# Dilated and grouped-query attentions: values as the stationary operand, probabilities moving, two heads in two column halves

## What is computed

```python
s = jnp.einsum('bhgqk,...')          # scores, query x key
p = jax.nn.softmax(s, axis=-1)       # divided by the row sum
o = jnp.einsum('bhgqk,bkhd->bqhgd', p, v)
```

## Time and profile before

| | us |
|---|---|
| median of 3 runs (2414.51 to 2415.35) | 2415.19 |
| the profiled execution, own time | 2413.57 |
| its span | 2411.8 |
| dilated attention, first scores to the next product | 875.0 to 979.2 |
| grouped-query attention, the same | 1553.2 to 1627.9 |

### The profile page before, as it was taken

One profiled execution on the slowest core, in us unless ns is written; L12 is line 12 of the kernel. 1 busy time (PEld: TensorE's weight loads), 2 busy tenths in 40 slices (PEclk: granted clock), 3 DMA queues, 4 the chain that ended last, 5 costly groups with the idle time before them and its releaser, 6 DMA issues.

```text
span 2411.8 us, 30157 instructions
## 1 busy us (share of the span) xinstructions
PE 2257.6 (94%) x11002; PEld 1858.1 (77%) x11002; DVE 1302.4 (54%) x1964; ACT 1106.8 (46%) x1646; POOL 54.1 (2%) x70
## 2 busy tenths in 40 slices
PE   7998899999999998999999998799999859999994
PEld 6876788888888876788888877678888648888883
DVE  3555663333365344453333477442355469898996
ACT  3435363433433246262442353352324348888884
POOL 1000000000000000000000000000000010000001
PEclk8999999999999999999999999999999979999997
DMA  5220233333223310243323232103323179999995
GB/s 167 88 79 27 79 105 97 97 97 98 91 79 96 96 45 1 79 130 97 96 87 105 79 116 82 60 1 105 96 70 105 57 284 397 409 410 408 407 404 188
DMA packets 129139, 338.60 MB, mean 140 GB/s; under 512 B 10528, under 2 KB 11712, under 8 KB 129040
## 3 DMA queue, kind: packets, MB, share of 16 engines
q1 hardware_dynamic: 117744, 296.85, 35.4%
q0 software_dynamic: 7840, 27.59, 3.4%
q10 hardware_dynamic: 3456, 12.81, 1.3%
HBM read 320.96 MB, written 16.25 MB: 140 GB/s over the span
## 4 chain that ended last, share of the span: by engine, by line
PE 84%; DVE 8%; ACT 4%; issue 1%; DMA 1%; POOL 0%; SPq 0%; ACTq 0%; DVEq 0%; POOLq 0%
PE bank L2136 40%; PE bank L2139 18%; PE bank L2485 10%; PE bank L2522 5%; PE bank L2243 3%; PE bank L2233 2%; PE bank L2223 2%; ACT arena L833 1%; DVE w_l L1261 1%; PE bank L2160 1%; PE bank L2465 1%; ACT w_h L795 1%; DMA X<-in_x_dram 1%; DVE stat L1293 1%; DVE xt_l L1328 1%
## 5 line engine op out<-in xcount | busy, mean ns | idle before, releaser
L1261 DVE TENSOR_TENSOR w_l<-w_raw,w_h 128x1024 fp32r<-128x1024 f32 x370 | 447.6, 1222 | 615.0 <-ACT w_h L795 612.0
L795 ACT CAST w_h<-w_raw 128x1024 fp32r<-128x1024 f32 x370 | 385.5, 1051 | 746.1 <-PE bank L2136 523.6
L2136 PE MATMUL bank<-w_h,xt_h 128*128 128x512 f32 (+1 forms) x960 | 378.9, 395 | 16.5 <-DVE w_l L1261 7.5
L2136 PE MATMUL bank<-w_l,xt_h 128*128 128x512 f32 (+1 forms) x960 | 373.7, 389 | 0.0
L2136 PE MATMUL bank<-w_h,xt_l 128*128 128x512 f32 (+1 forms) x960 | 373.6, 389 | 0.0
L2139 PE MATMUL bank<-xt_h,w_h 128*128 128x512 f32 x608 | 237.5, 391 | 8.1 <-DVE xt_l L1283 5.7
L2136 PE MATMUL bank<-w_h,ht_h 128*128 128x512 f32 x624 | 244.0, 391 | 0.7 <-DVE w_l L1261 0.7
L2136 PE MATMUL bank<-w_h,ht_l 128*128 128x512 f32 x624 | 242.9, 389 | 0.0
L1261 DVE TENSOR_TENSOR w_l<-spare,w_h 128x1024 fp32r<-128x1024 f32 x184 | 220.6, 1220 | 41.2 <-ACT w_h L795 40.4
L2136 PE MATMUL bank<-w_l,ht_h 128*128 128x512 f32 x624 | 242.8, 389 | 0.0
L2139 PE MATMUL bank<-xt_l,w_h 128*128 128x512 f32 x608 | 237.0, 390 | 0.0
(11 more groups left out here) (337 smaller groups left out, 2990.6 us busy)
## 6 DMA issues: line engine op xcount, KB each, us to landing
w_raw<-in_ffn_w_dram SPq DMA_DIRECT2D x128, 512.0 KB, 3.7
spare<-in_w_down_dram SPq DMA_DIRECT2D x92, 512.0 KB, 6.4
spare<-in_w_gate_dram SPq DMA_DIRECT2D x88, 512.0 KB, 6.8
w_raw<-in_w_up_dram SPq DMA_DIRECT2D x88, 512.0 KB, 6.4
w_raw<-in_w_in_dram SPq DMA_DIRECT2D x30, 512.0 KB, 3.8
w_raw<-in_ev_w_in_dram SPq DMA_DIRECT2D x28, 512.0 KB, 3.6
w_raw<-in_od_w_in_dram SPq DMA_DIRECT2D x24, 512.0 KB, 3.7
slot_y_dram<-slot_out ACTq DMA_DIRECT2D x23, 512.0 KB, 6.9
```

Source lines behind the costliest of these rows:

```text
L795: nc.scalar.copy(w_h[:, n % SLOTS, :], raw_of(n)).then_inc(sem("w_hi"), 1)
L1261: V.tensor_tensor(w_l[:, s_, :], raw_of(n), w_h[:, s_, :].bitcast(F32), ALU.subtract)\
L2136: mm = T.matmul(bank[set0 + m][:, 0:g.width], a[:, c, toks_of(m)], b[:, kk, :], start=first, stop=last)
```

## The change

Values become the stationary operand (128 keys x 64 channels) and the transposed probabilities the moving one (128 keys x 128 queries). The two heads of a step write rows 0 to 63 and 64 to 127 of the same bank, that is they use the two column halves of the array. The output comes out as [channel, query], so the four transposes per pair go. Four steps fill bank 6 (`V_BANK`), and the division by the sums is made once per pair: VectorE takes the reciprocals of the 8 sums, spreads them over 64 columns each, four products with the identity turn that into bank 7 (`B_BANK`), VectorE copies it to `work[:, 1]` and multiplies bank 6 by it into `work[:, 2]`. The high and low parts are then made from `work[:, 2]` in SBUF. `row_max`, `scores` and `trans` are moved out of `attention` unchanged, to be shared. `pair_start` counts the pairs for the new semaphores; the output semaphore of the two attentions is raised by 4 once per pair. The core of the diff:

```diff
+            def pairs(name, steps, probs, pt, work):            # ScalarE
+                def exps(k):
+                    if k % 4 == 0 and k >= 8:
+                        act.wait_ge(sem("at_inv"), h0 + k // 4 - 1)
+                    ...
+                for k in range(n + OT_LAG):
+                    if k < n:
+                        exps(k)
+                    if TRANS <= k < n + TRANS:
+                        t_, w = k - TRANS, steps[k - TRANS]
+                        act.wait_ge(sem("at_trans"), s0 + t_ + 1)
+                        if t_ >= 2:
+                            act.wait_ge(sem("at_values"), s0 + t_ - 1)
+                        nc.scalar.copy(pt[:, t_ % 2, :, 0:w.keys], banks[:, T_BANK:T_BANK + 2, 0:w.keys])\
+                            .then_inc(sem("at_ptcopy"), 1)
+                    if k >= 7 and k % 4 == 3:
+                        hp = (k - 7) // 4
+                        act.wait_ge(sem("at_out"), s0 + 4 * hp + 4)
+                        nc.scalar.copy(xt_or(name)[0][:, hp, :], work[:, 2, :]).then_inc(sem("ot_hi"), 1)
+            def pairs(name, steps, probs, work):                # VectorE
+                for k in range(n + OT_LAG):
+                    if k < n:
+                        row_max(s0, k, steps[k], probs)
+                    if k % 4 == 0 and k:
+                        hp = k // 4 - 1
+                        dve.wait_ge(sem("at_prob"), 2 * (s0 + k))
+                        if hp:
+                            dve.wait_ge(sem("at_spread"), h0 + hp)
+                        inv = inverse[:, hp % 2, :, :]
+                        own.do(V.reciprocal(inv, sums[:, 4 * (hp % 2):4 * (hp % 2) + 4, :]))
+                        V.tensor_copy(work[:, 0, :].rearrange("p (s c d) -> p s c d", s=4, c=2),
+                                      inv.unsqueeze(3).to_broadcast([P, 4, 2, 64])).then_inc(sem("at_inv"), 1)
+                    if k >= 7 and k % 4 == 3:
+                        hp = (k - 7) // 4
+                        dve.wait_ge(sem("ot_hi"), o0 + hp + 1)
+                        V.tensor_tensor(xt_or(name)[1][:, hp, :], work[:, 2, :], xt_or(name)[0][:, hp, :].bitcast(F32),
+                                        ALU.subtract).then_inc(sem("ot_lo"), 1)
+                    if k >= 6 and k % 4 == 2:
+                        hp = (k - 6) // 4
+                        dve.wait_ge(sem("at_spread"), h0 + hp + 1)
+                        own.do(V.tensor_copy(work[:, 1, :], bank[B_BANK][:, :]))
+                        dve.wait_ge(sem("at_values"), s0 + 4 * hp + 4)
+                        V.tensor_tensor(work[:, 2, :], bank[V_BANK][:, :], work[:, 1, :], ALU.mult)\
+                            .then_inc(sem("at_out"), 4)
+            def pairs(name, steps, probs, pt, work, warm):      # TensorE
+                for k in range(n + VALUES):
+                    if k < n:
+                        scores(s0, k, steps[k])
+                    if k == 3:
+                        keep_busy(warm, 16, B_BANK)
+                    if TRANS <= k < n + TRANS:
+                        t_ = k - TRANS
+                        trans(s0, t_, steps[t_], probs)
+                        if t_ % 4 == 3:
+                            hp = t_ // 4
+                            pe.wait_ge(sem("at_inv"), h0 + hp + 1)
+                            if hp:
+                                pe.wait_ge(sem("at_out"), s0 + 4 * hp)
+                            for i in range(4):
+                                mm = T.matmul(bank[B_BANK][:, toks_of(i)], work[:, 0, toks_of(i)], ident,
+                                              start=True, stop=True)
+                            mm.then_inc(sem("at_spread"), 1)
+                    if k >= VALUES:
+                        v_, w = k - VALUES, steps[k - VALUES]
+                        pe.wait_ge(sem("at_ptcopy"), s0 + v_ + 1)
+                        if v_ % 4 == 0 and v_:
+                            pe.wait_ge(sem("at_out"), s0 + v_)
+                        for b in range(w.keys // P):
+                            for c in range(2):
+                                mm = T.matmul(bank[V_BANK][rows_of(c), toks_of(v_ % 4)], w.values[c][b],
+                                              pt[:, v_ % 2, c, toks_of(b)], start=b == 0, stop=b == w.keys // P - 1)
+                        mm.then_inc(sem("at_values"), 1)
-            attention("dilated", dilated_steps, l_probs, l_pt, l_ot, tail1[0][0])
+            pairs("dilated", dilated_steps, l_probs, l_pt, l_work, tail1[0][0])
-            attention("gqa", gqa_steps, g_probs, g_pt, g_ot, m2_gates[0])
+            pairs("gqa", gqa_steps, g_probs, g_pt, g_work, m2_gates[0])
```

More of the change, by code:

```diff
@@ L600, in bass_two_blocks @@
         ot_chunks = {"dilated": 8, "gqa": 4, "cross": 4}
+        pair_start = {"dilated": 0, "gqa": 8}
+        B_BANK = 7
         TRANS, VALUES = 2, 3
@@ L1074, in _ @@
                             0.125 if k <= 2 else 1.0)
-            attention("dilated", dilated_steps, l_probs, l_pt, XT)
+            pairs("dilated", dilated_steps, l_probs, l_pt, l_work)
             tail(1, tail1)
@@ L1096, in _ @@
             transposed("sgu", HT)
-            attention("gqa", gqa_steps, g_probs, g_pt, HT)
+            pairs("gqa", gqa_steps, g_probs, g_pt, g_work)
             for k, g in enumerate(m2_gates):
@@ L1387, in attention @@
                 per = n // ot_chunks.get(name, 1)
[L1389 to L1404, removed]
                 def output(k):
@@ L1409, in output @@
                     if ot_dst is not None and k % per == 0 and k // per >= 2:
-                        dve.wait_ge(sem("ot_done"), ot.start[name] + k // per - 1)
+                        dve.wait_ge(sem("ot_done"), k // per - 1)
                     finish(k, steps[k], inv_sum[:, k % 2, :])
@@ L1762, in _ @@
                 evacuate(g, l_v, slice(k * HALF, (k + 1) * HALF))
-            attention("dilated", dilated_steps, l_probs, scaled, XT)
+            pairs("dilated", dilated_steps, l_probs, l_work)
             tail(1, tail1)
@@ L1821, in _ @@
             transposed("sgu", HT)
-            attention("gqa", gqa_steps, g_probs, scaled, HT)
+            pairs("gqa", gqa_steps, g_probs, g_work)
             for g in m2_gates:
@@ L2210, in keep_busy, with scores, trans @@
                     T.matmul(bank[spare][:, :], w[:, 0:P], w, start=True, stop=True)
+            def scores(s0, k, w):
+                for c, (q, key) in enumerate(w.scores):
+                    if k >= 2:
+                        pe.wait_ge(sem("at_prob" if w.mask is None else "at_max"), 2 * (s0 + k - 2) + c + 1)
+                    T.matmul(bank[2 * (k % 2) + c][:, 0:w.keys], q, key, start=True, stop=True)\
+                        .then_inc(sem("at_scores"), 1)
+            def trans(s0, k, w, probs):
+                if k >= 1:
+                    pe.wait_ge(sem("at_ptcopy"), s0 + k)
+                for c in range(2):
+                    pe.wait_ge(sem("at_prob"), 2 * (s0 + k) + c + 1)
+                    for b in range(w.keys // P):
+                        mm = T.transpose(bank[T_BANK + c][:, toks_of(b)], probs[:, k % 3, c, toks_of(b)], ident)
+                mm.then_inc(sem("at_trans"), 1)
             def attention(name, steps, probs, pt, ot_src=None, warm=None, extra=None):
@@ L2215, in attention @@
                 per = n // ot_chunks.get(name, 1)
[L2217 to L2234, removed]
                 def values(k):
@@ L2252, in attention @@
                     if TRANS <= k < n + TRANS:
-                        trans(k - TRANS)
+                        trans(s0, k - TRANS, steps[k - TRANS], probs)
                     if VALUES <= k < n + VALUES:
```

47 lines of the change are left out of this document (39 added, 8 removed).

## The result

| | before | after |
|---|---|---|
| median of 7 runs, us | 2415.19 | 2404.73 (2399.15 to 2408.65) |
| ratio | | 0.9954, 95% interval 0.9942 to 0.9966 |
| the profiled execution, own time | 2413.57 | 2406.70 |
| its span | 2411.8 | 2404.9 |
| dilated attention, first scores to the next product | 104.1 | 104.8 |

The change takes 10.5 us off, within 0.3 us of the 2405 on record. The stages of the profiled execution agree less well: the dilated attention, which was to give 3.9, takes 0.7 longer than before, so a right sum may hide wrong terms. The experiments are about that. The profiled execution is not a typical one: at 2406.70 it is the second longest of the seven.

The account below looks back on a forecast made before the run. The mask-exponential-copy chain was taken as the limit, tied with TensorE in the grouped-query attention. Dilated -3.9, grouped-query -4.9 and clock -1.0 gave -9.8 us: 2403.8 from 2413.57, 2405 for the median, range 2399 to 2410.

Parts of the forecast that it names:

- Price of the values: Values products in both attentions: 0.214 us per block plus 0.2 per step, 1.06 instead of 1.82 for 4 blocks.
- row halves: Scores of two heads in the trace, 0.214 us per block for both, taken as the price of column halves.
- The second rival: Between transposes, values and scores: every mode change drains TensorE, 0.4 instead of 0.2 us per step, 2411; chance 0.12.
- Spread: Once per pair, after the 384-key transposes: four full float32 products with two loads each, 0.93 us.
- The legs: Parts of a head pair: dilated 6.25, 3.14, 2.70 us, sum 12.09; grouped-query 3.98, 3.94, 3.05, 4.89, sum 15.86.
- the chain through ScalarE: Both attentions: scores, row maximum, two exponentials, copy, transposes; 4.11 us to dilated transposes, about 5.0 to the grouped-query copy's end.
- Cover for VectorE's work: Per pair, reciprocal (0.2 us) and broadcast (0.6) hide in VectorE's wait; copy and product leave 0.05 to spare.
- The sum: Dilated attention -3.9 us, grouped-query attention -4.9, clock -1.0, in all -9.8.
- the drain's term: End of the dilated attention: values stop waiting for scaling (0.68, 0.58 idle), last values 0.76 shorter, four transposes go: -1.5 us.
- The clock: After the grouped-query attention the gates' products lose 3 us at half clock; 1 us taken back.
- a rival of 0.08: Inside the attention, TensorE, idle for more of it, loses its clock: 2413 to 2420; chance 0.08.
- First rival: At the values: column halves don't overlap, 4 blocks cost 1.94 us, in sum +12.9, 2427; chance 0.14.

Follow-up runs that it names:

- the filled run: The changed kernel with products that nobody reads put into TensorE's waits in both attentions; 2403.9 us, ratio 0.9950 against the kernel before; measured again, 0.9959.

## Why the prediction was right

- **Price of the values.** Forecast 0.41, 0.63, 0.84 and 1.06 for 1 to 4 blocks, by analogy with row halves. Measured 0.37, 0.58, 0.81 and 1.03 to the next scores, plus some 0.09 ahead of them (953.76 to 954.12 is 0.36, before it was 0.28). So there are some 0.46 to 1.12: the slope is right, and a step costs some 0.05 more than forecast. The second rival, 0.2 more per step, is not there. The Trainium skill's rule that a change of tiling mode drains TensorE, in "TensorEngine Tiling (Array Packing)", Tiling Modes, fits the 0.09; that a drain is the reason is not shown by a run.
- **Spread.** 0.93 forecast; 0.98 measured (951.12 to 952.10), with the change to column halves inside.
- **The legs.** All seven, three dilated and four grouped-query, within 0.06 us. The limit of both attentions was named rightly: the chain through ScalarE. Its removal, and the transposes put into the wait, show it.
- **Cover for VectorE's work.** The broadcast takes 0.43, not 0.6, and is hidden; copy and product end in time.
- **The sum.** -3.9 and -4.9 by order, -1 by the clock: -9.8 against -10.5. Alone, the dilated attention gives 3.9 and the grouped-query one 7.2. That all this lies within 1.3 us is partly luck, since the terms are less good than their sum. With the clock held up to the drain, as in the filled run, the dilated attention is 2.7 us shorter than before (101.46 against 104.14), not 3.9. The round from the first scores to the 384-key scores of the second pair, booked at -0.34 like the others, is 0.28 longer (13.29 against 13.01), since no 512-key values stand in it and the spread does; the next six give 1.6, the end 1.3. The grouped-query attention without a fall is 5.6 shorter (69.13 against 74.69), not 4.9. And the 0.58 that the drain's term takes for a wait of values is the wait of the output transposes.
- **The clock** is the term that was not seen as it is. It was booked as one loss after the grouped-query attention with 1 us to win, and a fall inside was a rival of 0.08. In fact it falls inside the dilated attention in all four profiled executions in which TensorE waits 1.54 us in each dilated pair. That costs 1 and 3 us in the two of the changed kernel. In return the products after the grouped-query attention start at full clock, which is worth some 3 us, not 1; those after the dilated one do so too in the first profile, and are caught by a fall 1.4 us in (983.6) in the second. That gain and loss offset one another was not forecast. The step that failed is "204 to 208 was busy for only 2.94 of 4 us and kept 1.00", taken as a reason against the rival, with "some 72% of a dilated pair": one stretch that kept its clock says little, since stretches of 2.30 and 2.46 came ahead of falls and others of 2.09 and 2.35 did not. The share itself was misread too: 8.9 of 12.1 is 74%, and the pair measured has TensorE busy for 9.56 of 12.11 us, 79%, and still loses the clock.
- **First rival, its size.** 12.9 forecast and 12.8 measured (interval some 9 to 17), though only where both heads are truly in one half.

## What to carry to other kernels

Cut a pipelined stage into legs at the points where the limit changes hands, and price an edit leg by leg: 0.8 us off 16 records is worth that in one leg and nothing in the next. When a faster engine only waits longer, look at the order of the engine it waits for; here moving one copy ahead of two exponentials was worth more than the whole change and made the change worth 18 us instead of 10.5. Two narrow products overlap in full only if neighbours in the program lie in different halves of the array (1.03 us for 16 records, against 1.51 and 1.89), so make the loop over halves the inner one.

## What was not expected of the hardware

- Products of two column halves overlap in float32 (16 records in 1.10 us, 1.96 in one half) though both streams come from the same 128 partitions.
- With the halves one after the other, TensorE still overlaps part of them, 1.51 us: as the single records read, one of the second half starts while three of the first, earlier in the program, have not.
- The same kernel spreads more than the first runs let expect: 2399 to 2409 for the changed one, and 2410 to 2422 in 29 executions of the kernel before, whose first three lay within 0.9 us. The places at which the clock falls differ from one profiled execution of a kernel to the next (inside the dilated attention of the changed kernel at 907.7, 921.3 and 935.0, then at 911.9 and 949.5).
